# Where the modulation units and the first output-projection groups stand in two attention mixers

## The chip, the cores and the metric

One Trainium2 chip, one core. The kernel is a single launch; its time is device microseconds of that core, the median of three runs. TensorE (PE), ScalarE (ACT), VectorE (DVE), GpSimd (POOL) and the DMA queue of SyncE (SP) each take their instructions in program order and wait for each other on semaphores only. What is slow is therefore always one instruction at the head of an engine's queue, with everything behind it.

## The reference

The computation is three mixers in a row on 512 tokens of width 1024 (and, in the first two, 256 context tokens). Only the first two matter here:

```python
for i in range(2):                       # mixer A (i = 0), mixer B (i = 1)
    mod_x, mod_c = silu(c) @ w_mod[i] + b_mod[i], silu(c_ctx) @ w_mod[i] + b_mod[i]   # shift, scale, gate: 3 x 1024
    hx = rms_norm(x) * (1 + sc_x) + sh_x;  hc = rms_norm(ctx) * (1 + sc_c) + sh_c
    q, k, v, z = split(hx @ w_in)        # A: 16 query heads, 4 key heads, rope; B: 16 heads, window of the grid + bias
    o = softmax(q @ k.T * scale) @ v     # keys: tokens and context
    yx = (o * silu(z)) @ w_out
    x = x + g_x * yx                     # A also updates ctx, B does not
```

Then come a third mixer (recurrent heads and sparse attention) and a last norm, which the change leaves as they are.

## The kernel before

All weights go through one stream of units of 128 x 2048 numbers (1 MB each), in the order of `unit_order()`: unit n is loaded into buffer n % 2 of `W` when unit n - 2 has been used up. A projection in float32 is made of three fast matmuls: ACT rounds the weights to `WH`, POOL (or DVE) makes the rest `WL = W - WH` (`split`, four quarters a unit), and activations are kept as `HX`, `LX` (tokens) and `HC`, `LC` (context) in the same way. One slice `k` of a projection (`pj`) is WH*H, WH*L, WL*H. Modulation units (`mod_units`) are used as they are: `mod_mm` (16 matmuls from `W`), a copy of the sums by ACT (`mod_row`), `mod_tr` (4 small matmuls), one addition by DVE.

The order of the whole program is made by a planner in plain Python: `do(...)` appends an item, and every engine then walks the same list and issues its part of each item. In mixers A and B `attention()` interleaves two things. The steps are the attention itself: A has 48 steps, 8 pairs of heads by 6 tiles of 128 queries (tiles 0 to 3 have 768 keys, tiles 4 and 5 are context, with 256), B has 32, 8 pairs by 4 tiles with 512 keys. Step n issues the scores of n (PE), the softmax (DVE maximum, ACT exponential, DVE reciprocal, POOL scaling), the transposes of step n - 1 (`turn`) and the output of step n - 2 (`pv`). A generator, the fill, hands out projection work between these, at two places of each step: ahead of the second `turn` and ahead of the next step. A budget (`rate`, from `work` over the number of steps) says how much. `yield PAUSE`, or `yield -2`, ends the filling at this place, `until(...)` blocks it until a step has been planned.

```python
            def fill_in(n):
                debt[0] = min(debt[0], 60) + (rate * todo[n][2] if n < N else 0)
                while debt[0] > 0:
                    x = next(fill, None)
                    if x is None or x < 0:
                        break
                    debt[0] -= x
```

In A the fill is: for each pair the query projection (`gen_aq`, unit `aqz`, then the squares, sums and rope of the query), one modulation unit, the gate projection (`gen_az`); then three more modulation units and the activation parts of pairs 0 to 6. Parts (`parts`, by `parts_a`, `parts_b`) are what the output projection reads: ACT copies the gated attention output of pair k over slice k of HX and HC (possible only when the last gate projection has been read), and POOL (even k) or DVE (odd k) makes the low part. After the last step come the last gate, the parts of pair 7, two more modulation units, all splits of two weight units (`flush`), and then `out_proj`: the first two column blocks by both spans, four groups in four PSUM banks, first slices 0 to 5 of all, then 6 and 7 of each.

In B the fill is `gen_b(1)`, `gen_b(2)`, `gen_z(0)`, `gen_b(3)`, `gen_z(1..3)`, parts 0 to 5, where `gen_b(a)` projects queries, keys and values of the two pairs of group a and `gen_z(a)` their gates. `gen_b(a)` begins when group a - 2 is done with its buffers, `gen_z(a)` when group a is done. Its queries and keys have four buffers (`qB`, `kB`, by pair), its values two (`vB`, by group).

## Time and profile before

| what | value |
|---|---|
| runs | 1722.02 us median of 3 (1721.81 to 1722.54) |
| the profiled execution | 1719.79 us, of it 1718.1 us span |
| PE busy | 1584.9 us, 92% of the span |
| DVE, ACT, POOL busy | 729.3, 612.6, 643.1 us |
| mean granted TensorE clock | 0.954 |
| mixer A, first scores to last `pv` | 105.8 to 483.4 us |
| mixer B, first scores to last `pv` | 640.1 to 929.5 us |

The row of slices on the page gives each engine's busy share in tenths for 1/40 of the span (43 us); the row PEclk gives the granted TensorE clock. Where PE reads 9, the place is bound by TensorE; where it reads 5 to 8, TensorE waits for something, and a window of the trace tells for what.

### The profile page before, as it was taken

What the parts mean: (1) busy time and instruction counts of PE and PEld (TensorE: products, weight loads), DVE (VectorE), ACT (ScalarE), POOL (GpSimd) and SP (SyncE); (2) the same over time, 40 slices, a digit from 0 to 9 for tenths busy, and PEclk for the clock granted to TensorE, in tenths of its full rate; (3) what the DMA queues carried; (4) which work ended last, traced back from release to release, by engine and by line L of the source; (5) the groups of instructions that cost most, each with busy time, mean ns of one, the idle gap of its engine ahead of it and who ended that gap; (6) DMA issues with size and microseconds to landing.
All of it is one profiled execution on the core that took longest, in us unless ns stands there. A gap on an engine that the chain in (4) does not pass through costs nothing.

```text
span 1718.1 us, 25028 instructions
## 1 busy us (share of the span) xinstructions
PE 1584.9 (92%) x9858; PEld 1240.2 (72%) x9858; DVE 729.3 (42%) x1714; ACT 612.6 (36%) x1291; POOL 643.1 (37%) x640
## 2 busy tenths in 40 slices
PE   5899999999789799999997889999999898999997
PEld 3786677777568588788876668888887874555855
DVE  4344444444532624345355452524332374554033
ACT  4244444444522323333334342434332243333221
POOL 2433344342312434333343443435345242332352
PEclk8899999999979899999999889999998899999998
DMA  8111111111233222221221202122121221111221
GB/s 353 56 44 50 50 50 50 50 38 38 74 113 108 74 80 87 74 81 56 93 68 56 98 31 98 50 74 99 50 98 50 98 74 50 50 50 50 74 75 72
DMA packets 22148, 128.20 MB, mean 75 GB/s; under 512 B 2448, under 2 KB 2576, under 8 KB 8080
## 3 DMA queue, kind: packets, MB, share of 16 engines
q1 hardware_dynamic: 21888, 126.35, 20.6%
q8 instruction: 78, 1.28, 0.3%
q14 instruction: 38, 0.31, 0.1%
q10 hardware_dynamic: 144, 0.26, 0.1%
HBM read 124.50 MB, written 2.10 MB: 74 GB/s over the span
## 4 chain that ended last, share of the span: by engine, by line
PE 79%; DVE 9%; issue 4%; ACT 3%; POOL 3%; DMA 1%; DVEq 0%; POOLq 0%; SPq 0%; ACTq 0%
PE PS L1298 14%; PE PS L1300 14%; PE PS L1299 14%; PE PS L1379 6%; PE PS L1414 6%; PE PS L1389 5%; PE PS L1544 3%; PE PS L1293 3%; PE PS L1294 3%; PE PS L1295 3%; PE PS L1554 1%; DVE sm L1972 1%; POOL WL L2287 1%; ACT AR L1651 1%; DVE AR L2086 1%
## 5 line engine op out<-in xcount | busy, mean ns | idle before, releaser
L2287 POOL TENSOR_TENSOR WL<-W,WH 128x512 fp32r<-128x512 f32 x268 | 348.3, 1315 | 365.6 <-ACT WH L1574 365.3
L1298 PE MATMUL PS<-HX,WH 128*128 128x512 f32 x1008 | 414.7, 411 | 20.4 <-DVE LX L1895 16.9
L1300 PE MATMUL PS<-HX,WL 128*128 128x512 f32 x1008 | 398.1, 395 | 0.0
L1299 PE MATMUL PS<-LX,WH 128*128 128x512 f32 x1008 | 397.9, 395 | 0.0
L1298 PEld LDWEIGHTS PS<-HX,WH 128*128 128x128 f32 x1008 | 192.8, 191 | 68.9 <-issue 23.7
L1300 PEld LDWEIGHTS PS<-HX,WL 128*128 128x128 f32 x1008 | 192.0, 190 | 42.4
L1299 PEld LDWEIGHTS PS<-LX,WH 128*128 128x128 f32 x1008 | 192.8, 191 | 36.9 <-issue 1.9
L1574 ACT CAST WH<-W 128x512 fp32r<-128x512 f32 x296 | 171.0, 616 | 44.8 <-DMA W<-in_wu 37.4
L1651 ACT ACTIVATE AR<-PS,sm 128x768 f32<-128x768 f32 (+4 forms) x160 | 115.7, 723 | 177.8 <-DVE sm L1977 105.3
L1972 DVE TENSOR_REDUCE sm<-PS 128x1 f32<-128x512 f32 (+4 forms) x224 | 149.9, 669 | 42.5 <-PE PS L1379 38.1
L2343 POOL TENSOR_SCALAR AR<-AR,sm 128x768 f32<-128x768 f32 (+1 forms) x96 | 73.4, 764 | 220.8 <-DVE sm L1988 220.8
L1379 PE MATMUL PS<-AR 64*128 64x256 f32 (+3 forms) x704 | 126.9, 468 | 11.1 <-ACT XC L1651 5.2
L1414 PE MATMUL PS<-AR 128*64 128x128 f32 x1408 | 103.1, 295 | 21.9 <-DVE AR L1997 13.1
L1414 PEld LDWEIGHTS PS<-AR 128*64 128x64 f32 x1408 | 82.5, 146 | 49.8 <-issue 30.4
L1379 PEld LDWEIGHTS PS<-AR 64*128 64x128 f32 x704 | 61.0, 189 | 64.7 <-issue 41.5
L1389 PE MATMUL PS<-C,AR 128*128 128x128 f32 x608 | 101.8, 287 | 4.5 <-DVE AR L2008 4.1
L2343 POOL TENSOR_SCALAR XC<-XC,sm 128x512 f32<-128x512 f32 x64 | 44.8, 700 | 160.1 <-DVE sm L1988 160.1
L1661 ACT COPY AR<-PS 128x512 f32<-128x512 f32 (+1 forms) x112 | 62.1, 554 | 116.0 <-PE PS L1389 115.6
L1389 PEld LDWEIGHTS PS<-C,AR 128*128 128x128 f32 x608 | 70.1, 144 | 40.4 <-issue 25.1
L1293 PE MATMUL PS<-WH,HX 128*128 128x256 f32 x320 | 96.6, 302 | 2.6 <-POOL WL L2287 2.6
L1651 ACT ACTIVATE XC<-PS,sm 128x512 f32<-128x512 f32 x64 | 44.2, 690 | 149.1 <-DVE sm L1977 149.1
L1294 PE MATMUL PS<-WH,LX 128*128 128x256 f32 x320 | 93.2, 291 | 0.0
(268 smaller groups left out, 2488.4 us busy)
## 6 DMA issues: line engine op xcount, KB each, us to landing
W<-in_wu SPq DMA_DIRECT2D x98, 1024.0 KB, 4.8
AR<-in_wu SPq DMA_DIRECT2D x8, 1024.0 KB, 11.0
AR<-in_biasb SPq DMA_DIRECT2D x32, 256.0 KB, 2.7
XX<-in_xt SPq DMA_DIRECT2D x2, 1024.0 KB, 6.1
out<-XX SPq DMA_DIRECT2D x8, 256.0 KB, 2.2
XC<-in_xt SPq DMA_DIRECT2D x1, 1024.0 KB, 14.4
C<-in_cc SPq DMA_DIRECT2D x1, 770.5 KB, 8.6
CS<-in_cs SPq DMA_DIRECT2D x1, 512.0 KB, 9.9
```

Of the source, the lines that this page charges most:

```text
L1293: e.matmul(o, xh, wh, start=(k == 0), stop=False)
L1294: e.matmul(o, xl, wh, start=False, stop=False)
L1298: e.matmul(o, wh, xh, start=(k == 0), stop=False)
L1299: e.matmul(o, wh, xl, start=False, stop=False)
L1300: t = e.matmul(o, wl, xh, start=False, stop=(k == 7))
L1379: t = e.matmul(PS[:, s.score[h] + a:s.score[h] + b], l, r, start=True, stop=True)
L1389: t = e.transpose(o[:, j * 128:j * 128 + 128], s.pb[h][:, (q0 + j) * 128:(q0 + j) * 128 + 128], c("id"))
L1414: t = e.matmul(s.out[h], s.values[h][j], s.pt[h][:, j * 128:j * 128 + 128], start=(j == 0 and s.first), stop=(j == nv - 1 and s.final))
L1574: e.copy(WH[:, PART[n], a:z], W[:, n % 2, a:z]).then_inc(*s_wh.by(n, q))
L1651: e.activation(s.pb[h][:, 0:s.n], PS[:, s.score[h]:s.score[h] + s.n], ACT.Exp, bias=smn[:, i % 4:i % 4 + 1], scale=(1.0 if s.scale is None ...
L1972: e.tensor_reduce(mx, x, AX.X, ALU.max).then_inc(*s_max.by(name, n, h))
L2287: e.tensor_tensor(WL[:, d, a:z], W[:, n % 2, a:z], WH[:, d, a:z].bitcast(F32), ALU.subtract).then_inc(*s_wl_pool.by(n, q))
```

## The change

Mixer A: the modulation units are no longer fill of their own. `gen_aq` and `gen_az` take a second generator, `ride`, and step it once after each of their two spans: `mod_mm` and `mod_row` after the first, `mod_tr` after the second, so that a span's projection lies between the copy and the matmul that reads it. All twelve units of the fill ride in pairs 0 to 6 in this way (in `unit_order()` they stand between the `aqz` units accordingly); none is left behind the last step. In both mixers the output projection's first two column blocks of the token span begin within the fill (`begin_out`): after the parts of pairs 0, 1, 2 comes slice 0 of both, and so on to slice 6, each slice two behind the parts. After the last step follow the parts of pair 7, in A the two context groups (slices 0 to 6), then slice 7 of each. `flush()` ahead of the output projection is gone. Mixer B: queries and keys of pair m may be written when pair m - 4 is done, values of group a when pair 2a - 3 is done; the gates of group a come ahead of `gen_b(a + 2)` and no longer wait for the group's steps, as `b_gated` is issued when both the gate and the pair are there.

```diff
-    u = [("ak",), ("av",), ("aqz", 0)]
-    for i in range(7):
-        u += [("aqz", i + 1), m[i]]
-    u += m[7:12]
+    u = [("ak",), ("av",), ("aqz", 0), m[0]]
+    for i in range(1, 8):
+        u += [("aqz", i)] + m[2 * i - 1:2 * i + 1 if i < 6 else 12]
...
-        def gen_aq(pair, pr):
+        def gen_aq(pair, pr, ride=iter(())):
...
                 do("a_query_raw", pair, j)
+                next(ride, None)
                 yield PAUSE
...
+        def begin_out(name, phase, part, done, pr):
+
+
+            un = Unit(name, 0)
+            led = {(m, 0): bank(pr.take((name, m, 0), (s_res, (name, m, 0)))) for m in (0, 1)}
+            for k in range(9):
+                if k < 7:
+                    yield from until(lambda: k in done)
+                    part(k)
+                    yield 3
+                if k >= 2:
+                    for m in (0, 1):
+                        yield from pj((name, m, 0), un, 0, T, 128 * m, phase, led[m, 0], (k - 2,))
+            begun[name] = un, led
...
         def fill_a():
+            riding = iter(MA[:12])
...
             for pair in range(8):
                 if pair:
-                    yield from gen_aq(pair, FA)
-                    yield from mod_units(MA[pair - 1][0], (MA[pair - 1][1],), FA)
-                if pair < 7:
-                    yield from gen_az(pair, FA)
-            yield from gen_az(7, FA)
-            for l, u in MA[7:10]:
-                yield from mod_units(l, (u,), FA)
-            yield from parts_a(range(7))
+                    yield from gen_aq(pair, FA, ride())
+                yield from gen_az(pair, FA, ride())
+            yield from begin_out("aout", "o", parts_a, done_a, FA)
...
-        run(parts_a(range(7, 8)))
-        for l, u in MA[10:12]:
-            run(mod_units(l, (u,), FA))
-        flush()
+        LEAD = ring((2,), (3,))
+        parts_a(7)
...
         def gen_b(a, pr):
-            yield from until(lambda: a < 2 or a - 2 in done_b)
             for m in (2 * a, 2 * a + 1):
+                yield from until(lambda: m < 4 or m - 4 in pairs_b)
...
+            yield from until(lambda: a < 2 or 2 * a - 3 in pairs_b)
             un = Unit("bv", a)
...
-            yield from until(lambda: a == 3 or a in done_b)
+            yield from until(lambda: not a or 2 * a - 1 in gated_b)
...
-                  chain(gen_b(1, FB), gen_b(2, FB), gen_z(0, FB), gen_b(3, FB), gen_z(1, FB), gen_z(2, FB), gen_z(3, FB), parts_b(range(6))), 8 * (3 * (4 * T + 2 * LC + 6 * 256) + 8 * T) / 100 + 6 * 5,
+                  chain(gen_b(1, FB), gen_z(0, FB), gen_b(2, FB), gen_z(1, FB), gen_b(3, FB), gen_z(2, FB), gen_z(3, FB),
+                        begin_out("bout", "p", parts_b, gated_b, FB)), 8 * (3 * (4 * T + 2 * LC + 6 * 256) + 8 * T + 14 * T / 8) / 100 + 7 * 3,
                   posted_b, scored_b)
-        for m in (6, 7):
-            do("b_gated", m)
-        run(parts_b(range(6, 8)))
-        flush()
+        parts_b(7)
```

Where the instructions stand. TensorE in A, the end of step 43 and step 44 before: L1379 are scores (two spans, two heads), L1414 is `pv`, L1389 the transposes of one head, L1311 a `mod_mm`, L1320 its `mod_tr`.

```order
L1379 MATMUL PS<-AR 128x512 x2
L1379 MATMUL PS<-AR 128x256 x2
L1414 MATMUL PS<-AR 64x128 x12
L1389 MATMUL PS<-C,AR 128x128 x6
L1311 MATMUL PS<-W,sm 32x256 x8
L1389 MATMUL PS<-C,AR 128x128 x6
L1320 MATMUL PS<-C,AR 128x2 x2
```

TensorE in A with the change, step 42: L1398 are its scores, L1433 the `pv` of step 40, L1408 the transposes of step 41, and L1317 to L1319 slice 0 of the output projection for the first and the second column block.

```order
L1398 MATMUL PS<-AR 128x512 x2
L1398 MATMUL PS<-AR 128x256 x2
L1433 MATMUL PS<-AR 64x128 x4
L1408 MATMUL PS<-C,AR 128x128 x2
L1317 MATMUL PS<-HX,WH 128x512
L1318 MATMUL PS<-LX,WH 128x512
L1319 MATMUL PS<-HX,WL 128x512
L1317 MATMUL PS<-HX,WH 128x512
L1318 MATMUL PS<-LX,WH 128x512
L1319 MATMUL PS<-HX,WL 128x512
L1408 MATMUL PS<-C,AR 128x128 x2
```

So the modulation unit with its pair of matmuls has left this place, and the first output-projection slice now stands between the two transposes of a step, ahead of the second one.

ScalarE in A before, the end of the attention: L1615 are the copies of the parts (the last of the fourteen of pairs 0 to 6, then the two of pair 7), L1661 copies of transposes, L1651 exponentials, L1581 the modulation copies, L1574 the rounding of weights.

```order
L1615 CAST HC<-AR 128x256
L1661 COPY AR<-PS 128x512
L1651 ACTIVATE AR,sm<-PS,sm 128x256 x2
L1661 COPY AR<-PS 128x256 x2
L1615 CAST HX<-AR 128x512
L1615 CAST HC<-AR 128x256
L1581 COPY AR<-PS 128x256 x2
L1574 CAST WH<-W 128x512 x8
```

ScalarE in A with the change, step 42 and the beginning of step 43: the same copies of parts are L1634, the exponentials L1670, the copies of transposes L1680.

```order
L1670 ACTIVATE AR,sm<-PS,sm 128x768 x2
L1634 CAST HX<-AR 128x512
L1634 CAST HC<-AR 128x256
L1634 CAST HX<-AR 128x512
L1634 CAST HC<-AR 128x256
L1634 CAST HX<-AR 128x512
L1634 CAST HC<-AR 128x256
L1680 COPY AR<-PS 128x256
L1634 CAST HX<-AR 128x512
L1634 CAST HC<-AR 128x256
```

The fourteen copies stood in one block behind the exponentials of step 46 before; they now come in blocks of six, two, two, two and two, behind the exponentials of steps 42 to 44, and the eight roundings of weights and the modulation copies behind the last step are gone from there.

ScalarE in B with the change, steps 28 to 31: L1634 parts, L1670 exponentials (two heads), L1680 copies of transposes, L1593 the rounding of the next unit's weights.

```order
L1670 ACTIVATE XC,sm<-PS,sm 128x512 x2
L1634 CAST HX<-AR 128x512 x4
L1680 COPY AR<-PS 128x512
L1634 CAST HX<-AR 128x512
L1670 ACTIVATE XC,sm<-PS,sm 128x512 x2
L1634 CAST HX<-AR 128x512
L1593 CAST WH<-W 128x512 x2
L1634 CAST HX<-AR 128x512
L1680 COPY AR<-PS 128x512
L1670 ACTIVATE XC,sm<-PS,sm 128x512 x2
```

Before, the first six parts stood behind the exponentials of step 30 (two, a copy of a transpose, four); now the first five stand behind those of step 28.

## Rows read from the trace of the kernel before

**Rows 1.** The page: busy time of TensorE, its clock by slices, and one group.

```profile
PE 1584.9 (92%) x9858; PEld 1240.2 (72%) x9858; DVE 729.3 (42%) x1714; ACT 612.6 (36%) x1291; POOL 643.1 (37%) x640
PE   5899999999789799999997889999999898999997
PEclk8899999999979899999999889999998899999998
...
L2287 POOL TENSOR_TENSOR WL<-W,WH 128x512 fp32r<-128x512 f32 x268 | 348.3, 1315 | 365.6 <-ACT WH L1574 365.3
```

**Rows 2.** Windows: from:to length, busy of each engine, granted clock, DMA share, GB/s.

```profile
105.78:431.42 325.64, 306.23 (x2370) 234.61 (x2371) 150.57 (x417) 139.82 (x300) 124.05 (x126) 0.98 0.13 46
431.42:483.37 51.95, 36.75 (x314) 25.82 (x313) 27.54 (x65) 23.63 (x54) 18.70 (x20) 0.84 0.17 62
483.37:491.65 8.28, 5.77 (x42) 3.06 (x41) 3.46 (x9) 3.02 (x7) 0.00 (x0) 0.50 0.60 192
491.65:511.19 19.54, 19.54 (x96) 16.70 (x97) 6.00 (x10) 3.86 (x8) 0.00 (x0) 0.85 0.38 134
...
700.34:723.49 23.15, 19.77 (x113) 15.62 (x112) 8.84 (x26) 7.20 (x16) 7.85 (x8) 0.85 0.07 23
723.49:912.15 188.66, 188.66 (x1393) 157.47 (x1392) 91.99 (x240) 69.35 (x159) 72.00 (x75) 1.00 0.22 76
912.15:929.48 17.33, 8.23 (x74) 6.54 (x73) 9.02 (x20) 7.99 (x17) 8.51 (x8) 0.80 0.18 61
...
929.48:973.30 43.82, 43.81 (x194) 35.95 (x192) 18.30 (x27) 18.22 (x32) 16.48 (x13) 1.00 0.21 72
```

**Rows 3.** Waits of TensorE in 105.78:437.1: us in total, times, longest.

```profile
PE PS L1414 <- DVE AR L1997: 5.2, 6, 1.0
PE PS L1364 <- ACT AR L1633: 4.5, 3, 1.7
...
PE PS L1320 <- ACT AR L1581: 3.0, 2, 1.5
```

**Rows 4.** Timeline of TensorE in A, steps 43, 44: start, length, instruction [idle before].

```profile
437.12 1.56 PE L1379 MATMUL PS<-AR 64*128 64x512 f32 x8
...
447.98 1.07 PE L1311 MATMUL PS<-W,sm 128*32 128x256 f32 x16
448.98 0.87 PE L1389 MATMUL PS<-C,AR 128*128 128x128 f32 x6
451.15 0.58 PE L1320 MATMUL PS<-C,AR 128*128 128x2 f32 x4 [1.29 <-ACT AR L1581]
```

**Rows 5.** Timeline of TensorE in A, behind the scores of step 47.

```profile
474.15 2.83 PE L1414 MATMUL PS<-AR 128*64 128x128 f32 x24 [7.88 <-DVE AR L1997]
...
483.37 1.93 PE L1311 MATMUL PS<-W,sm 128*32 128x256 f32 x16
```

**Rows 6.** Timeline of ScalarE in A: the second exponential of step 42.

```profile
435.90 0.99 ACT L1651 ACTIVATE AR<-PS,sm 128x768 f32<-128x768 f32 x1 [0.56 <-DVE sm L1981]
```

**Rows 7.** Timeline of POOL and of DVE: low parts of activations.

```profile
466.01 1.26 POOL L2317 TENSOR_TENSOR LX<-AR,HX 128x512 fp32r<-128x512 f32 x1 [0.59 <-ACT HX L1615]
...
468.62 1.75 DVE L1902 TENSOR_TENSOR LX<-AR,HX 128x512 fp32r<-128x512 f32 x1
...
485.18 0.69 DVE L1902 TENSOR_TENSOR LX<-AR,HX 128x512 fp32r<-128x512 f32 x1 [0.35 <-ACT HX L1615]
```

**Rows 8.** Timelines in B: scores of steps 8, 29, 30, an exponential, `pv` of step 30.

```profile
706.90 2.08 PE L1379 MATMUL PS<-AR 64*128 64x256 f32 x8 [3.38 <-ACT XC L1651]
...
899.65 1.13 PE L1379 MATMUL PS<-AR 64*128 64x256 f32 x8
905.00 0.20 ACT L1651 ACTIVATION_READ_ACCUMULATOR XC<-PS,sm 128x1 f32 x1
908.27 1.13 PE L1379 MATMUL PS<-AR 64*128 64x256 f32 x8
...
923.96 1.97 PE L1414 MATMUL PS<-AR 128*64 128x128 f32 x16 [4.57 <-ACT AR L1661]
```

More of the change, by code:

```diff
@@ L58, in unit_order @@
     for a in range(4):
+        u += [("bz", a - 2)] if a >= 2 else []
         u += [("bqk", 2 * a), ("bqk", 2 * a + 1), ("bv", a)]
-        u += [("bz", a - 2)] if a >= 2 else []
     u += [("bz", 2), ("bz", 3)]
@@ L717, in gen_aq, with gen_az @@
             yield PAUSE
-        def gen_az(pair, pr):
+        def gen_az(pair, pr, ride=iter(())):
             un = aun[pair]
@@ L724, in gen_az @@
                 do("a_gate", pair, j)
+                next(ride, None)
                 yield PAUSE
@@ L786, in build @@
         unv.done(s_proj, "av", 5)
-        attention("a", [s for pair in range(8) for s in steps_a(pair)], SA, TA, PbA, PTbA, OA, fill_a(), 8 * 15 * (T + LC) / 100 + 14 * 5, posted_a)
+        attention("a", [s for pair in range(8) for s in steps_a(pair)], SA, TA, PbA, PTbA, OA, fill_a(), (8 * 15 * (T + LC) + 14 * T) / 100 + 7 * 3, posted_a)
         do("a_last_gate")
@@ L795, in out_proj @@
             for u in range(4):
[L796 to L797 removed]
                 if u == 0:
[L799 to L802 removed]
+                    un, led = begun[name] if name in begun else (Unit(name, 0), {})
+                    for j, (lo, hi) in enumerate(spans):
+                        for m in (0, 1):
+                            if (m, j) not in led:
+                                led[m, j] = bank(LEAD.take((name, m, j), (s_res, (name, m, j))))
+                                run(pj((name, m, j), un, lo, hi, 128 * m, phase, led[m, j], range(7)))
+                else:
+                    un = Unit(name, u)
                 for m in (2 * u, 2 * u + 1):
@@ L896, in gen_z, with gated, parts_b @@
                 do("b_gate", m)
-                if a < 3:
-                    do("b_gated", m)
+                gates_b.add(m)
+                gated(m)
                 yield 3
             un.done(s_proj, "bz", 2 * a + 1)
-        def parts_b(ks):
-            for k in ks:
-                parts("p", k, 0, zB[:, k, :], [(s_gated, ("b", k)), (s_proj, ("bz", 7))], "pool" if k % 2 == 0 else "dve")
-                yield 5
+        def gated(m):
+            if m in gates_b and m in pairs_b:
+                do("b_gated", m)
+                gated_b.add(m)
+        def parts_b(k):
+            parts("p", k, 0, zB[:, k, :], [(s_gated, ("b", k)), (s_proj, ("bz", 7))], "pool" if k % 2 == 0 else "dve")
         def load_bias(n):
```

42 lines of the change are left out of this document (19 added, 23 removed).

## The prediction

> **What bounds the kernel now.** I read the page first: TensorE is busy 92% of the span, and its row of slices reads 9 nearly everywhere but in a few dips, two of which lie where mixers A and B end, near 470 and 920 us; the clock row dips with it [rows 1]. So I asked for windows around these two ends, then for the waits and the timelines inside them.
>
> In A, from the first scores to those of step 42, TensorE is busy 306 of 326 us. Then it thins out: 36.8 of 52.0 us to the last `pv`, at a granted clock of 0.84, then 5.8 of 8.3 us in the last two modulation units at 0.50, then the first four output groups in 19.5 us at 0.85 [rows 2]. The end of these four groups, 511.19, is my mark of A. In B TensorE is full from 723 to 912 us. Ahead of that, the 23 us of steps 7 to 9 hold 3.4 us of idle at a clock of 0.85; behind it, 17.3 us hold 8.2 us of work. From 929.48 on it is full again [rows 2]: eight groups of eight slices in 43.8 us, 0.68 us a slice. My mark of B is the end of the first two output groups: sixteen slices, 940.4.
>
> So TensorE's own work sets the time nearly everywhere, and the change issues the same matmuls. All there is to win or lose is idle time and half-speed time: 19.4, 15.2, 2.5, 3.4 and 9.1 us of idle in these windows, 50 in all.
>
> **A, before step 42.** Five more modulation units now lie here (twelve for seven), and the second half of the last gate projection. A unit costs 1.0 us (`mod_mm`, to the transposes behind it) and 0.58 us (`mod_tr`) [rows 4], so 7.9 us; the projection's context span is 8 slices of half of 0.68, 2.7 us. Together +10.6. What goes: the waits for the modulation copy, 3.0 us, since a span's projection now lies ahead of `mod_tr`, and most of the 4.5 us that the query's sums wait for ACT, since in pairs 1 to 6 a `mod_tr` stands ahead of them; I take 3. The 5.2 us behind copies of transposes stay [rows 3]. A clock of 0.98 over 326 us is 6.5 us of full speed missing [rows 2], and it drops behind idle; I let 4 come back. What comes: the fill is less even. In the planner's new list the steps of tile 0 of pairs 3 to 6 get only 1.5, 0.8, 0.4 and 0 us of fill, at the prices above. Such a step needs 2.6 us of TensorE for itself (scores 1.5, context `pv` and transposes 1.1, estimated from a third of a full one), and step 42, the like of it, takes 5.7 us from 431.42 to 437.12 [rows 2, 4], with its fill. If 5.5 is the floor, 1.4 + 2.1 + 2.5 + 2.9 = 9 us are new idle. Against it, three steps that were thin, the ones behind the old modulation units, are full now; -3. Sum: 10.6 - 3 - 3 - 4 + 9 - 3 = +6.6. A second count, step by step (a step's work or its floor, plus the excess that its kind has in the trace), gives +4. I take +4, nearer to the count that uses more rows: the scores of step 42 at 435.5. The ends are 0 and +9.
>
> **A, from step 42 to the mark.** Before: 511.19 - 431.42 = 79.8 us. After:
> Step 42. The first slice waits for its part: the second exponential ends 5.5 us behind the scores' start (436.9) [rows 6], the copy takes 0.6, the low part by POOL 1.26 [rows 7]: 7.4 us, while TensorE is through with scores, `pv` and transposes after 2.4. A wait of 5.0 us. Then four slices, 2.7 us, and a transpose: 10.3. In B, 3.4 us of idle are followed by scores at half speed, 2.08 us for 1.13 [rows 8], so I add 1.5: 11.8.
> Step 43 holds three slices, and its chain sets it: 7. In step 44 the low parts of pair 5 on DVE stand ahead of its maximum, at 1.75 us for 512 columns with POOL at work, not 0.69 [rows 7]: 8. Step 45: 7. Step 46, short and without fill: 5.5. From the `pv` of step 45 to the end of the last one it took 9.2 us (474.15 to 483.37) at half speed [rows 5]; with the scores of step 47 ahead, 9.8. The 7.88 us that this `pv` waited behind fourteen copies of parts [rows 5] is gone. Sum 49.1.
> Then the context groups, 14 slices of 0.34, and slice 7 of all four: 6.8 us at full speed. The last gate and the parts of pair 7 lie beneath them, 3 us if they didn't. The old window from 491.65 lost 0.15 x 19.5 = 2.9 us to the clock [rows 2]; so does this: 9.7.
> 58.8 instead of 79.8: -21.0. With +4 ahead of it A gains 17.0.
>
> **B.** Steps 7 to 9: `bz` 0 waits for nothing now, and pair-wise buffers let the next projections follow. The 3.4 us of idle [rows 8] and the half speed, 0.15 x 23.15 = 3.5 us [rows 2], go: -6.9.
> The end: all gates are planned by step 27, not 30. So at the scores of step 28 the kernel has done what it had done at 912.15, less three attentions of 3.15 us (a step of 8.62 us, 899.65 to 908.27, less eight slices) [rows 8]: 902.7 on the old clock. From there to the mark took 37.7 us. After: step 28 waits for its first part as A does: exponentials end 5.55 us behind the scores (905.20) [rows 8], copy 0.6, POOL 1.3: 7.45, a wait of 4.8 us behind 2.6 us of work. Six slices and a transpose make 11.9, half speed 12.9. Step 29: slice 5 waits for part 5, 1.9 us, and slice 6 for part 6, whose low part stands on POOL behind two quarters of weights of 1.3 us [rows 1], 1.5 us: 11.2. Step 30: 5.5. Step 31: exponentials 5.5, then scaling, transposes, copy and `pv`, 3.3 as an estimate (rows 5 hold this piece twice in 9.2 us at half speed). Then nothing covers gate and part of pair 7, 2.3 us, where six slices a group did; two slices, 1.4. Sum 42.1, +4.4, though the 4.57 us behind the parts [rows 8] are gone. B gains 2.5.
>
> **Weights.** Without `flush` POOL spreads the next unit's splits, and the unit after is loaded some 10 us later against A's mark, and needed 12 us later still. I count 0; without that cover it is one load, under 5 us.
>
> **Sum.** -17.0 - 2.5 = -19.5. The profiled execution would go from 1719.8 to 1700.3, and the median, 2.2 us above it, from 1722.0 to 1702.5; I say 1703.
>
> **A rule against the change.** Low parts take 1.75 us on DVE beside POOL and 0.69 alone [rows 7]. My price for it is the 1 us more in step 44; paid in all five steps with parts, 42 to 44, 28 and 29, it is 5.
> The Trainium skill (SBUF — State Buffer, "Who interferes with whom") says that a DVE tensor_tensor with both inputs in SBUF contends with GpSimd's reads. By that rule, which the trace bears out, parts among the steps slow both engines that the softmax needs; it is part of rival 2.
>
> **The rivals.**
> 1. The ends close up further: the first slices wait 2 us instead of 5, and A's thin steps cost nothing. A 4 + 3 more, B 3 more: 1693. For it: TensorE's work alone would allow it. Against: both waits are read off a chain. 0.20.
> 2. The parts press on DVE and POOL: 5 us as above, and the clock is at half through both ends, 3 us more each: 1703 + 11 = 1714. For it: rows 7, and 0.50 in the old window from 483. 0.15.
> 3. Slower. TensorE stands in order: a slice that waits delays the transposes and scores behind it, these the next exponentials, and behind those stands the next part. If the other twelve parts wait too (three do in my sum), it decides from 19.5 / 12 = 1.6 us each; at 2.3 us it is 1703 + 28 = 1731. For it: parts are issued behind the exponentials of their step. Against: a slice stands two parts behind. 0.04.
> 4. The change doesn't do what it says: the waits only move into thin steps of A (+9 there, 13 less at its end), and B's end eats what step 8 gives: 1719 to 1723. 0.04.
> My forecast, 1697 to 1709: 0.57.
>
> **Range.** 1691 to 1714, with rival 1 and nearly all of rival 2. 0.2% (3.4 us) is about what a measurement can tell from no change. Faster 0.92, same 0.04, slower 0.04.
>
> **What would show it.** A: `mod_tr` without waits; scores of step 42 near 435; ahead of the first output slice a wait of 4 to 5 us for POOL's low part, and none near 7.9 us behind it; the mark near 494. B: no idle in steps 7 to 9 and a clock of 1.00 there; a wait of 4 to 5 us in step 28, two smaller ones in step 29, one of 2 us ahead of slice 7; the time between the marks 2 to 3 us shorter. It is wrong if A's thin steps lose more than 9 us, if the first waits drag the steps behind them, or if the clock stays at half through both ends, which the sum has at 1.5 and 2.9 us in A and 1 in B.
> The Trainium skill (TensorE: Matmul & The Clock Gate, "HAM oscillation — how this bites in real kernels") says that bursts with pauses between them bring the clock down again and again. The trace agrees behind the 3.4 us in B.

## The result: slower, where faster was predicted

The changed kernel takes 1755.69 us (median of 4 runs, 1747.64 to 1756.69) against 1721.91 us for the one before (1720.25 to 1722.54): a ratio of 1.0191, with a 95% interval of 1.0169 to 1.0212. Predicted were 1703 us, with a range of 1691 to 1714. The profiled execution took 1756.69 us, of it 1755.0 us span.

Its page, the rows that answer to [rows 1]: busy time, TensorE and its clock in 40 slices, the splits by POOL.

```profile
PE 1600.5 (91%) x9858; PEld 1250.6 (71%) x9858; DVE 718.1 (41%) x1702; ACT 612.4 (35%) x1291; POOL 658.7 (38%) x652
PE   5899987888979799999997978999999898999997
PEclk8899999899999899999998888999998899999998
L2306 POOL TENSOR_TENSOR WL<-W,WH 128x512 fp32r<-128x512 f32 x280 | 364.1, 1315 | 348.3 <-ACT WH L1593 348.3
```

The number of matmuls is the same, and TensorE is busy 16 us longer. The sixth to the tenth slice of TensorE, 220 to 440 us, were all 9 and now read 8, 7, 8, 8, 8: that is the body of A, not its end. The windows say how much. They answer to [rows 2]: A's first scores to those of step 42; on to the mark of A; B's first scores to those of step 28; on to the sums of the norm behind B's output projection (they stood at 975.61 before).

```profile
105.00:483.42 378.42, 335.23 (x2494) 254.25 (x2495) 152.02 (x423) 143.30 (x310) 128.24 (x129) 0.93 0.16 56
483.42:537.25 53.83, 44.16 (x325) 32.77 (x325) 27.55 (x70) 25.44 (x57) 22.45 (x24) 0.94 0.01 4
661.17:924.65 263.48, 263.48 (x1913) 221.02 (x1912) 119.51 (x326) 98.17 (x223) 103.82 (x108) 1.00 0.22 77
924.65:1011.84 87.19, 68.40 (x362) 53.63 (x361) 38.17 (x72) 32.03 (x63) 32.42 (x29) 0.86 0.16 53
```

| stretch | before | predicted change | after | measured change |
|---|---|---|---|---|
| A, scores of step 0 to step 42 | 325.6 | +4 | 378.4 | +52.8 |
| A, step 42 to its mark | 79.8 | -21.0 | 53.8 | -26.0 |
| B, scores of step 0 to step 28, same work before it | 269.4 | -6.9 | 263.5 | -5.9 |
| B, on to the norm's sums | 72.9 | +4.4 | 87.2 | +14.3 |

The third row of before is 902.7 less 633.3, the last 975.6 less 902.7, with the place 902.7 as the prediction worked it out (the work that the changed kernel has behind it at its step 28). The last column sums to 35.2; with 1.8 between the mark of A and B's first scores it is the 36.9 us of the span, but for a tenth. The prediction's +4.4 ended at its mark of B, 940.4; that stretch took 50.2 us in the change for 37.7, +12.5, and the rest of the +14.3 lies behind the mark. So two of four terms were right or better, one was 10 off, and one was off by 49.

What A's body waits for, TensorE in 105:483.4 (answers to [rows 3]); the waits of `mod_tr` for its copy are gone, as predicted. Transposes waited 3.8 us before, scores 2.4; the waits of projections (L1317) are new. The query's sums (L1383, 4.5 before) and `pv` (L1433, 5.2 before, 2.1 now) wait a little less.

```profile
PE PS L1408 <- DVE AR L2027: 11.4, 10, 3.1
PE PS L1317 <- POOL WL L2306: 8.2, 5, 1.8
PE PS L1398 <- ACT AR L1670: 8.1, 4, 2.2
PE PS L1317 <- DVE AR L1951: 4.5, 3, 2.2
PE PS L1317 <- DVE AR L1971: 4.2, 4, 1.6
PE PS L1383 <- DVE AR L1951: 3.9, 2, 2.1
```

In words: transposes (L1408) wait for the output's scaling on DVE; projections (L1317) for POOL's splits, and for DVE's copies of a query (L1951) and of a gate (L1971) out of the PSUM bank that they are to use; scores (L1398) for the exponential. Idle is 378.42 - 335.23 = 43.2 us for 19.4 before; and a clock of 0.93 over 378 us is about 26 us of full speed missing for 6.5. These two make some 43 of the 52.8; the added work of five units and half a projection was put at 10.6.

The largest single wait, 3.05 us, comes three times (steps 22, 28, 34). Here around step 28, the timeline of TensorE:

```profile
359.85 1.53 PE L1433 MATMUL PS<-AR 128*64 128x128 f32 x24
361.31 0.66 PE L1408 MATMUL PS<-C,AR 128*128 128x128 f32 x4
365.01 0.44 PE L1408 MATMUL PS<-C,AR 128*128 128x128 f32 x2 [3.05 <-DVE AR L2027]
```

DVE in the same time:

```profile
359.22 0.69 DVE L1962 TENSOR_TENSOR AR<-PS,CS 128x512 f32<-128x512 f32 x1
363.48 0.69 DVE L1965 TENSOR_TENSOR AR<-AR 128x512 f32<-128x512 f32 x1 [3.57 <-POOL AR L2355]
...
364.68 0.28 DVE L2027 SCALAR_TENSOR_TENSOR AR<-PS,AR 128x128 f32<-128x128 f32 x1
```

And POOL:

```profile
358.99 2.28 POOL L2350 TENSOR_TENSOR sm<-sm 128x12 f32<-128x12 f32 x1
361.25 0.90 POOL L2362 TENSOR_SCALAR AR<-AR,sm 128x768 f32<-128x768 f32 x1
362.12 1.26 POOL L2355 TENSOR_TENSOR AR<-AR,CS 128x512 f32<-128x512 f32 x1
```

Read it from the bottom. POOL takes the root of the query's sums (2.28), a scaling of the softmax (0.90), and then its part of the query's rotation (`a_query_rope`, 1.26). DVE stands 3.57 us for that part, inside its own part of the rotation. Behind the rotation in DVE's order are the maximum of the new scores and the scaling of the output of two steps ago (L2027), which empties bank 5; and the next transpose goes into bank 5. TensorE has 2.8 us of work, then nothing, and the seven slices that were to fill this step stand behind that transpose. The clock falls behind it: 0.75 over the 6.7 us from 365.01. Windows of the wait and of what follows:

```profile
361.90:365.01 3.11, 0.06 (x1) 0.00 (x0) 1.44 (x4) 0.80 (x2) 1.48 (x2) 1.00 0.00 0
365.01:371.72 6.71, 6.71 (x23) 5.35 (x24) 1.04 (x4) 1.60 (x5) 1.75 (x2) 0.75 0.00 0
```

### The profile page after: what moved, and what is told of

It is laid out like the page before. It is cut to its first block, busy times and chain, and to the rows that moved or that the text cites. A ratio compares the mean times of both kernels' runs of the same rounds, so it can differ in the third digit from the quotient of the medians.

```text
span 1755.0 us, 25015 instructions
## 1 busy us (share of the span) xinstructions
PE 1600.5 (91%) x9858; PEld 1250.6 (71%) x9858; DVE 718.1 (41%) x1702; ACT 612.4 (35%) x1291; POOL 658.7 (38%) x652
## 4 chain that ended last, share of the span: by engine, by line
PE 77%; DVE 10%; issue 4%; POOL 4%; ACT 3%; DMA 1%; DVEq 0%; POOLq 0%; SPq 0%; ACTq 0%
PE PS L1317 14%; PE PS L1318 13%; PE PS L1319 13%; PE PS L1398 6%; PE PS L1433 6%; PE PS L1408 6%; PE PS L1563 3%; PE PS L1312 3%; PE PS L1313 3%; PE PS L1314 3%; DVE sm L1991 2%; POOL WL L2306 2%; PE PS L1573 1%; DMA W<-in_wu 1%; PE PS L1330 1%
## 5 line engine op out<-in xcount | busy, mean ns | idle before, releaser
L2306 POOL TENSOR_TENSOR WL<-W,WH 128x512 fp32r<-128x512 f32 x280 | 364.1, 1315 | 348.3 <-ACT WH L1593 348.3
L1317 PE MATMUL PS<-HX,WH 128*128 128x512 f32 x1008 | 422.1, 419 | 44.1 <-DVE LX L1914 17.2
L1318 PE MATMUL PS<-LX,WH 128*128 128x512 f32 x1008 | 403.5, 400 | 0.0
L1319 PE MATMUL PS<-HX,WL 128*128 128x512 f32 x1008 | 403.0, 400 | 0.0
L1317 PEld LDWEIGHTS PS<-HX,WH 128*128 128x128 f32 x1008 | 196.5, 195 | 95.7 <-issue 35.0
L1319 PEld LDWEIGHTS PS<-HX,WL 128*128 128x128 f32 x1008 | 195.5, 194 | 43.5
L1593 ACT CAST WH<-W 128x512 fp32r<-128x512 f32 x296 | 171.5, 616 | 49.5 <-DMA W<-in_wu 42.1
L1670 ACT ACTIVATE AR<-PS,sm 128x768 f32<-128x768 f32 (+4 forms) x160 | 115.5, 722 | 192.6 <-DVE sm L1996 105.4
L1398 PE MATMUL PS<-AR 64*128 64x256 f32 (+3 forms) x704 | 127.6, 470 | 13.8 <-ACT AR L1670 11.2
L1680 ACT COPY AR<-PS 128x512 f32<-128x512 f32 (+1 forms) x112 | 62.1, 554 | 161.5 <-PE PS L1408 161.3
L1408 PE MATMUL PS<-C,AR 128*128 128x128 f32 x608 | 105.5, 294 | 13.2 <-DVE AR L2027 11.7
L1398 PEld LDWEIGHTS PS<-AR 64*128 64x128 f32 x704 | 61.4, 191 | 70.0 <-issue 41.7
L1408 PEld LDWEIGHTS PS<-C,AR 128*128 128x128 f32 x608 | 72.3, 148 | 49.4 <-issue 26.1
L1433 PE MATMUL PS<-AR 128*64 128x128 f32 x1408 | 99.5, 288 | 8.0 <-ACT AR L1680 7.9
L1433 PEld LDWEIGHTS PS<-AR 128*64 128x64 f32 x1408 | 79.2, 142 | 35.3 <-issue 31.6
L1670 ACT ACTIVATE XC<-PS,sm 128x512 f32<-128x512 f32 x64 | 44.1, 689 | 151.4 <-DVE sm L1996 151.4
## 6 DMA issues: line engine op xcount, KB each, us to landing
CS<-in_cs SPq DMA_DIRECT2D x1, 512.0 KB, 10.4
```

What stands on the lines that cost most here:

```text
L1317: e.matmul(o, wh, xh, start=(k == 0), stop=False)
L1318: e.matmul(o, wh, xl, start=False, stop=False)
L1319: t = e.matmul(o, wl, xh, start=False, stop=(k == 7))
L1398: t = e.matmul(PS[:, s.score[h] + a:s.score[h] + b], l, r, start=True, stop=True)
L1408: t = e.transpose(o[:, j * 128:j * 128 + 128], s.pb[h][:, (q0 + j) * 128:(q0 + j) * 128 + 128], c("id"))
L1433: t = e.matmul(s.out[h], s.values[h][j], s.pt[h][:, j * 128:j * 128 + 128], start=(j == 0 and s.first), stop=(j == nv - 1 and s.final))
```

## The experiments

For each run the table gives the stretches of its profiled execution, by the starts of scores and of the norm's sums: A0-42 and A0-24 from A's first scores to those of step 42 and 24; 42-B on to B's first scores; B0-28; 28-N on to the norm's sums; the rest. The ratios are to runs of the kernel before taken beside each run, whose medians lie between 1720.2 and 1722.5 us.

| run | A0-24 | A0-42 | 42-B | B0-28 | 28-N | rest | median us | ratio (95%) |
|---|---|---|---|---|---|---|---|---|
| before | 186.9 | 325.6 | 201.9 | 257.7 | 84.6 | 742.5 | | |
| the change | 219.5 | 378.4 | 177.8 | 263.5 | 87.2 | 743.1 | 1755.7 | 1.0191 (1.0169-1.0212) |
| 1 ride only | 184.7 | 335.5 | 185.5 | 258.2 | 84.7 | 740.1 | 1713.6 | 0.9950 (0.9932-0.9968) |
| 2 no ride | 194.9 | 346.6 | 191.3 | 263.5 | 88.0 | 741.5 | 1740.2 | 1.0123 (1.0085-1.0161) |
| 3 all of B | 186.7 | 326.8 | 201.7 | 263.5 | 88.1 | 740.4 | 1728.1 | 1.0029 (1.0015-1.0043) |
| 4 B's order | 186.7 | 326.7 | 201.7 | 262.9 | 86.2 | 741.1 | 1726.4 | 1.0027 (1.0014-1.0039) |
| 5 change, A's old number | 184.7 | 334.8 | 179.6 | 263.5 | 87.8 | 741.3 | 1715.5 | 0.9962 (0.9944-0.9979) |
| 6 before, A's new number | 194.9 | 349.6 | 201.6 | 257.8 | 84.6 | 742.5 | 1742.2 | 1.0113 (1.0088-1.0139) |
| 7 A only, old number | 184.7 | 336.7 | 179.3 | 258.2 | 84.8 | 740.9 | 1706.1 | 0.9914 (0.9894-0.9933) |
| 8 B spread | 186.8 | 325.5 | 201.9 | 258.4 | 81.7 | 738.3 | 1712.5 | 0.9947 (0.9929-0.9964) |
| 9 A old, B spread | 184.7 | 335.9 | 180.5 | 258.4 | 79.2 | 745.1 | 1702.6 | 0.9892 (0.9874-0.9911) |
| 10 change, A 1000 | 200.0 | 363.3 | 180.1 | 263.5 | 85.2 | 739.7 | 1739.4 | 1.0113 (1.0096-1.0130) |
| 11 A 960, B spread | 196.3 | 338.8 | 178.0 | 258.4 | 79.0 | 739.3 | 1700.7 | 0.9888 (0.9873-0.9902) |
| 12 A old, B 1200 | 184.7 | 334.2 | 180.6 | 261.0 | 85.9 | 740.2 | 1710.5 | 0.9943 (0.9929-0.9958) |
| 13 change, rotation later | 209.9 | 360.2 | 179.4 | 263.5 | 87.3 | 745.2 | 1743.5 | 1.0133 (1.0094-1.0172) |
| 14 no ride, rotation later | 186.8 | 322.8 | 191.5 | 263.5 | 87.8 | 740.7 | 1716.4 | 0.9970 (0.9955-0.9985) |
| 15 as 14, B spread | 189.7 | 325.8 | 191.2 | 258.4 | 80.1 | 741.0 | 1703.7 | 0.9892 (0.9875-0.9908) |

In the rows of before, 1, 6 and 7, B0-28 has 17 slices less in it than in the change, and 28-N that much more: for B compare the two together, 342.3 us before and 350.7 in the change. Where B is spread (8, 9, 11, 15) some slices are shifted in the same way, and where A's number differs the work done by step 24 or 42 differs a little: the change has 24 more small matmuls (eight context slices, some 3 us) behind it at step 42 than run 5.

**Runs 1 to 4: the parts alone.** My first theory was the one that the waits for PSUM banks suggest: that the riding units break the order of the two banks that A's projections take in turn, and lose its body by themselves. Run 1 is the kernel before with riding alone.

```diff
+                next(ride, None)      # in gen_aq and gen_az, behind each span
...
-                    yield from mod_units(MA[pair - 1][0], (MA[pair - 1][1],), FA)
```

> The kernel before with one part of the change: the modulation units ride on A's projections (with the order of the weight units that goes with it), no output slices in the fill, B as before. Theory 1, riding itself lengthens A's body (one PSUM bank is asked for again right behind each projection, weights of the next pair are split late, and the idle brings the clock down): scores of step 42 some 50 us later than before (near 484), TensorE's waits there 40 us and more, and since two modulation units behind the last step are gone, 30 to 45 us slower in all. Theory 2, the body is lengthened by something else of the change: step 42 within 10 us of 435, and the time within 10 us of before.

It is faster, 0.9950: the theory falls. Riding alone adds 9.9 us to A's body, about the 10.6 of the added work, and takes 16.4 off behind it. Run 2 is the change without riding (the old places of the units, all twelve in the fill).

> The change without riding: A's modulation units are fill of their own as before (all twelve ahead of the output slices), everything else of the change stays. Theory 1: scores of step 42 back at 431 (+-2), the time 25 to 50 us below the changed kernel. Theory 2: step 42 stays above 470. As the five late units take one step each, the output slices come only in step 47, so the end of A is worth less than in the change: its mark (end of the first four output groups) 505 to 515, as before.

It is slow, 1.0123, and has lost 21.0 us in A's body with no unit more there up to pair 7. Neither theory has it right: step 42 starts at 450.5, between the 431 of the one and the 470 of the other, and the time is 15 us below the change, not 25 to 50. So something else that the change brings slows A's body by itself. Run 3 has the A of before and all of B's part; run 4 of that only the pair-wise buffers and the earlier gates, with no output slice in the fill.

```diff
-chain(gen_b(1, FB), gen_b(2, FB), gen_z(0, FB), gen_b(3, FB), gen_z(1, FB), gen_z(2, FB), gen_z(3, FB), parts_b(range(6))) ...
+chain(gen_b(1, FB), gen_z(0, FB), gen_b(2, FB), gen_z(1, FB), gen_b(3, FB), gen_z(2, FB), gen_z(3, FB), parts_b(range(6))) ...
```

> A as before, B as in the change (buffers by pair, gates earlier, output slices in the fill). The two traces give B as 8 us longer (36.2 us late behind B against 27.9 ahead of it). If that is B's own doing: 1722 + 8 = 1730. If it came from what A left behind: 1716 to 1720.

> A as before; of the change in B only the buffers by pair and the earlier gates, the parts and the output projection behind the last step as before. My reading of the two traces: the idle and the half clock of steps 7 to 9 go and nothing is added, 6 to 7 us faster (1715). Rival: B's end becomes worse also without the output slices, since all fill is gone by step 28 and the last steps are bare: 1720 to 1724.

Both lose, 5 us by the ratios, run 4 against my own reading that it would gain 6 to 7; B takes 351.6 and 349.1 us for 342.3. The idle of steps 7 to 9 is gone in both, and both lose more than that at the end, run 4 with no output slice at all among the steps. TensorE there, in steps 29 to 31:

```profile
902.82 1.13 PE L1384 MATMUL PS<-AR 64*128 64x256 f32 x8 [1.81 <-ACT XC L1656]
905.85 1.98 PE L1419 MATMUL PS<-AR 128*64 128x128 f32 x16 [1.90 <-ACT AR L1666]
...
921.51 1.90 PE L1384 MATMUL PS<-AR 64*128 64x256 f32 x8 [2.50 <-ACT XC L1656]
...
929.30 1.98 PE L1419 MATMUL PS<-AR 128*64 128x128 f32 x16 [2.98 <-ACT AR L1666]
```

The `pv` take 1.98 us, where that of step 28 took 1.09. The gates that had covered these steps are done earlier, so the steps stand bare: the scores of steps 29, 30 and 31 each wait for an exponential (1.8, 3.4 and 2.5 us), and the granted clock is 0.84 over the 86.2 us, so that 27 us of them run at half clock. The 3.4 us of idle in step 8 had not been removed; they had been moved to the end, where they came back larger.

**Runs 5 and 6: one number.** In A the change also altered the last argument of `attention`, the work that the fill is said to hold: 1014.3 for 991.6, which gives each half step 11.74 units instead of 11.48. Run 5 is the whole change with the old number, run 6 the kernel before with the new one.

```diff
-        attention("a", ..., (8 * 15 * (T + LC) + 14 * T) / 100 + 7 * 3, posted_a)
+        attention("a", ..., 8 * 15 * (T + LC) / 100 + 14 * 5, posted_a)
```

> The change with one number put back: the work that attention A is told its fill holds, 991.6 as before instead of 1014.3. It sets how much fill each half step gets (11.48 and 11.74 units). The planner's lists say that with 1014.3 the fill of a pair runs out before the pair's last step is over: it meets its own gate (the query projection of pair p waits for pair p-2) in steps 18, 24, 30 and 36, and step 36 gets none; with 991.6 it never does. Theory R (the faster supply lost A's body): steps 0 to 42 take 335 to 340 us instead of 378, as in the kernel with riding alone (335.5), the waits of 3.05 us ahead of the transposes and of 2.2 us ahead of the scores go, and the clock is near 0.98; the end of A stays at 178 us to B's first scores, B stays at 351 us to the norm sums: 1712 to 1719 us. Theory S (riding together with the early output slices loses it, whatever the rate): 1745 to 1756.

> The kernel before with one number changed, A's fill told as 1014.3 instead of 991.6; nothing else. Theory R: the same gates are met in steps 18, 24, 30 and 36 as in the change; steps 0 to 42 take 342 to 350 us instead of 326 (the kernel without riding took 346.6), with three or four waits of 3 us ahead of the transposes and as many of 2.2 us ahead of scores; the end is at most 4 shorter: 1733 to 1745 us. Theory S (the rate is no cause): 1720 to 1724.

Both come out in the ranges of theory R, though its reason for them falls below: run 5 gets 40 us of the median back (43.6 in A's body of the profiled executions), and run 6 loses 20 to 24 with nothing else changed. TensorE's waits in the body of run 5, the largest of its kinds:

```profile
PE PS L1317 <- POOL WL L2306: 5.8, 5, 1.2
PE PS L1433 <- ACT AR L1680: 3.6, 1, 3.6
PE PS L1383 <- DVE AR L1951: 2.8, 2, 1.4
...
PE PS L1408 <- DVE AR L2027: 1.9, 6, 0.3
```

and its window:

```profile
106.70:441.50 334.80, 313.57 (x2470) 238.19 (x2471) 152.35 (x422) 141.34 (x308) 127.08 (x128) 0.98 0.17 61
```

The wait for the output's scaling (L1408) is 1.9 us for 11.4, idle is 21.2 for 43.2, and the clock is back at 0.98.

**Runs 7 and 8: the parts that pay.** Run 7 has A of the change with the old number, and B as before. Run 8 has A as before and all of B's part, with one number: B's fill is said to hold 1060 units, not 1403. The values of the next pairs are then pulled in where they are needed, and what is left lasts through step 31, with five to six slices a step.

```diff
-begin_out("bout", "p", parts_b, gated_b, FB)), 8 * (3 * (4 * T + 2 * LC + 6 * 256) + 8 * T + 14 * T / 8) / 100 + 7 * 3,
+begin_out("bout", "p", parts_b, gated_b, FB)), 1060,
```

> Mixer A as in the change (units ride, first output groups among the last steps) but with the old 991.6, mixer B as before. Theory R with theory E (A's end gives what was predicted, 178 us from step 42 to B's first scores for 186 with riding alone): B's first scores at 619 to 622, B 342.5 to the norm sums: 1703 to 1709 us, some 7 below the kernel with riding alone. If the early output slices cost on DVE and POOL what they save, it is 1711 to 1715, the same as riding alone.

> Mixer A as before, mixer B as in the change, with one number: the work that attention B is told its fill holds, 1060 instead of 1403. By the planner's list the fill, which ended in step 30 with one slice, lasts through step 31 with 5 to 6 slices a step, since the values of pairs 2, 4 and 6 are then pulled in at once where they are needed. Theory T (B's end is lost because steps 28 to 31 have too little work of TensorE in them, and the clock falls behind their waits): step 28 to the norm sums takes 75 to 79 us instead of 88, the time up to step 28 grows by at most 4 less what moved: together 340 to 345 us for 351.6, 1716 to 1722 us. Theory U (the waits for the first parts, and DVE and POOL busy with parts, lose it): 1725 to 1730, as with the number of the change.

Run 7 is as expected, 1706.1. Run 8, 1712.5, is faster than expected, though step 28 to the norm's sums takes 81.7 us, not 75 to 79; of the 14.5 us that its span is below that of run 3, 11.5 lie in B (340.1 for 351.6) and 2.1 in the rest, where the two programs are the same.

**Runs 9 to 12: together, and sizes between.** Run 9 puts both numbers into the change; 10 gives A 1000; 11 is run 9 with A at 960; 12 is run 9 with B at 1200.

> The change with both numbers: A's fill told as 991.6, B's as 1060. If the two losses are separate, it has the A of the run with A alone (1706 where before was 1722.5) and the B of the spread fill (10 below before): 1694 to 1700 us. If the two share something (the state of the clock, the weights that are loaded ahead), it is 1702 to 1710.

> The change with A's fill told as 1000, between 991.6 and 1014.3. By the planner's list the fill meets its gate in steps 30 and 36 alone. Theory R (what costs is the fill standing at its gate and the lumps behind it): up to the scores of step 24 A runs within 3 us of the kernel with 991.6, and loses 10 to 25 us from there to step 42: body 345 to 360, in all 1725 to 1740 us. Theory P (what costs is the rate itself, more fill in each half step): the loss grows evenly from step 0, 16 us in all, 7 to 9 of them before step 24.

> Both numbers again, but A's fill told as 960: the fill lags a half step behind that with 991.6 in most pairs, meets no gate, and lasts through step 47 with one slice left over. If only gates matter, A's body is 334 to 340 us as with 991.6, and the end gains what the steps 46 and 47 now cover, 1 to 3 us: 1692 to 1700. If a lagging fill brings waits of its own (the rope of a pair late for its first scores), 1703 to 1712.

> Both numbers, A 991.6, B's fill told as 1200: it ends with one slice in step 31, where 1060 holds 6 slices in step 31 and the number of the change ends in step 30. Theory T (what the last steps hold of TensorE's work decides): between the two, step 28 to the norm sums 83 to 87 us, and 3 to 8 us over the run with 1060. Theory U (waits for parts decide): as with the number of the change, 87 to 88.

Run 9 misses its 1694 to 1700 by 3: B's part gives 5.5 us over run 7 (337.5 for 343.0 in B), and the profiled execution loses 4 in the rest, where the code is that of run 7. Windows of run 9, its B and the piece of B from step 28:

```profile
622.50:960.00 337.50, 325.82 (x2273) 269.05 (x2273) 158.02 (x398) 129.19 (x286) 137.62 (x136) 0.99 0.22 74
880.80:960.00 79.20, 67.53 (x385) 52.87 (x385) 38.02 (x73) 33.46 (x66) 37.22 (x33) 0.98 0.17 58
```

TensorE's waits in the second:

```profile
PE PS L1317 <- POOL LX L2336: 6.9, 2, 4.8
PE PS L1317 <- DVE LX L1921: 1.7, 1, 1.7
PE PS L1433 <- ACT AR L1680: 0.8, 1, 0.8
```

The two waits for POOL's parts are the same 6.9 us as in the change; what went are most of the waits of the bare steps and of the half clock, 0.98 for 0.86. So theory T holds and U doesn't: the parts cost little beyond their waits. Run 12 lies between, as T has it.

Run 11, at 960, meets no gate either and has a body of 338.8 us; its 1700.7 us are the least of all runs, though run 9 can't be told from it by the intervals. But its first half shows that a lower number is not harmless: with less work done by step 24 it takes 196.3 us to get there, where 991.6 takes 184.7, and projections wait 9.4 us for the copy of a gate (L1971) out of their bank, for 1.0 in run 5. It gets most of this back behind step 24. So the time does not simply rise with the number; what counts is how the fill falls among the steps.

Run 10 is where theory R as I had put it fails. I had taken the loss for the fill standing at its own gate (`until`, the pair before last must be done). By the planner's list that happens in steps 18, 24, 30 and 36 with 1014.3, in 30 and 36 with 1000. But run 10 has lost 15 us by step 24. Nor does P hold, which wants an even loss of half that. Run 10 is within 0.2 us of run 5 at the scores of step 14; then a query's context slices come in two pieces, five in step 14 and three in 15, where run 5 has all eight in 15. TensorE of run 10 behind that:

```profile
232.32 1.99 PE L1383 MATMUL PS<-C,AR 128*128 128x2 f32 x12 [1.41 <-DVE AR L1951]
234.25 1.22 PE L1398 MATMUL PS<-AR 64*128 64x256 f32 x4
235.40 2.83 PE L1433 MATMUL PS<-AR 128*64 128x128 f32 x24
```

The query's sums wait for the copy of slices that ended just ahead of them, and the following scores and `pv` run at half clock (2.83 for 1.53). There the two lists differ in where the modulation unit and the first five context slices fall: a half step earlier in run 10.

**Runs 13 and 14: the rotation's place.** Both keep 1014.3 and all four stands at the gate. They add a pause that lets the query's rotation be planned in the first half of a step only.

```diff
...
             do("a_query_sums", pair)
             yield PAUSE
+            if pair and half[0]:      # half[0]: 1 in the second filling of a step
+                yield PAUSE
...
```

What the planner's list has for pair 4 (slices in the first and the second half of the step):

```
            the change               run 13                  run 5
step 21     sums   | rotation        sums     |              8        | sums
step 22     7      | 1               rotation | 8            rotation | 6
```

> The change with its 1014.3 and one more pause: the rotation of a pair's queries is planned in the first half of a step only. By the planner's list this moves those of pairs 4, 5 and 6 from the second half of steps 21, 27, 33 to the first half of steps 22, 28, 34, and the stands at the gate in steps 18, 24, 30 and 36 stay as they are. Theory Q (rotation ahead of the scores of a short step: its additions stand ahead of the output's scaling on DVE): the three waits of 3.05 us go and with them the half clock behind each, 5 to 6 us each: body 360 to 364 us instead of 378, 1737 to 1742 us. Theory G (the gate and the lumps behind it): 1750 to 1756.

> The same pause in the kernel without riding (1740 us, body 346.6, of which 21 are over the kernel before). Theory Q: its three waits of 3.05 us go, body 329 to 333, 1722 to 1727 us. Theory G: 1736 to 1741.

Theory Q holds in both. Run 13's body is 360.2 us, 18.2 less. The three waits of 3.05 us are gone. But not all of the 18.2 is the rotation: up to step 21 the change and run 13 issue the same instructions in the same order, and the change is 4.5 us behind there already (189.6 for 185.1), at a clock of 0.95 for 0.97: so much two executions can differ where nothing in them does. 13.7 us lie behind; steps 22, 28 and 34 alone give 10.4. The medians are 12.2 us apart, and their intervals just meet. Run 14 has 322.8, 24 less than run 2 (2.7 of it ahead of step 21) and less than the kernel before, with every stand at the gate still there: so without riding these stands cost nothing. The body of run 13:

```profile
106.00:466.20 360.20, 323.00 (x2495) 245.76 (x2496) 152.24 (x423) 143.01 (x310) 128.66 (x129) 0.97 0.17 59
```

and that of run 14:

```profile
103.80:426.60 322.80, 305.14 (x2394) 235.56 (x2394) 151.29 (x418) 140.37 (x300) 124.41 (x126) 0.99 0.14 47
```

Run 13 still has 25.4 us more than run 5. TensorE's waits in its body:

```profile
PE PS L1403 <- ACT AR L1675: 11.3, 8, 2.2
PE PS L1322 <- POOL WL L2311: 8.5, 5, 1.9
PE PS L1322 <- DVE AR L1956: 4.5, 3, 2.2
PE PS L1322 <- DVE AR L1976: 4.2, 4, 1.6
PE PS L1388 <- DVE AR L1956: 3.9, 2, 2.1
...
PE PS L1413 <- DVE AR L2032: 2.2, 7, 0.5
```

The wait behind the rotation (transposes, L1413) is 2.2 us for 11.4. The largest of the list, scores for exponentials, is 8.1 in the change; but it is not what sets run 13 apart from run 5, for these two differ by 25.2 us ahead of step 24 and by 0.2 behind it. Ahead of step 24 run 13 idles 20.8 us for 5.5, and of the 15.3 more, 13.0 are waits for splits (4.9 for 3.5), for banks (8.7 for 1.0) and of the query's sums for a copy (3.9 for none). The waits for splits and for banks, which run 14 doesn't have, have this reason: the riding unit takes the bank between a projection's two spans, so the second span finds its own bank not yet copied out when nothing else lies between.

**Run 15: the rest together.** The A of run 14 and the B of run 8.

> No riding, rotations in first halves, A's fill told as 1014.3, B's as 1060. If the two add up: the run without riding and with the later rotation was 4.6 below before, B's fill spread takes 337 to 340 us to the norm sums instead of 351: 11 to 14 less, so 1702 to 1706 beside a before of 1721. If B's part gives only the 4 us that it gave in the run with both old numbers: 1711 to 1714. The tail behind the norm sums 739 to 742 us as in nearly all runs, if the 745 of the run with both old numbers was that execution's own.

1703.7, with 741.0 in the rest. Runs 9, 11 and 15 are alike, 1.1% below the kernel before, with units that ride and without.

## Why the prediction was wrong, by its steps

**A, before step 42** ("I take +4") is the step that failed: +52.8. The runs take it apart, each piece one difference of the table:
- 9.2 us is riding and the added work, at the old number (run 5 less before). That was put at 10.6, and the waits of `mod_tr` did go. Of the 3 us taken off for the query's sums only 0.6 came: they waited 4.5 us before and 3.9 in the change.
- 18.2 us is the change less run 13. 13.7 of it lie behind the place where the two first differ and are the rotation, one half step too early in three pairs, give or take the 3 us or so by which executions differ; the other 4.5 lie ahead of it.
- 25.4 us comes with riding at the new number (run 13 less run 5, all of it ahead of step 24; seven context slices that run 5 does later, some 2.4 us, are in it); without riding, the same number and the same gates cost nothing (run 14 less before, -2.8). That the waits for splits and banks, and the clock behind them (0.98 for 1.00 up to step 24), make it up is read off the waits and not tried by itself.

I had the planner's list and counted in it only how much of TensorE's work each step holds, and took 9 us for the steps of tile 0 that get little. These, the stands at the gate, cost nothing by run 14, which has no riding; with riding they were not tried apart. What I didn't look at was in what order the query's copies, sums and rotation fall among the steps. Steps and fill share DVE's and POOL's queues, and there a rotation is a chain over POOL, 4.4 us from the root to the product in the rows above. [Rows 3] have such chains, 1 us each behind copies of DVE; I carried them over as they were. "I let 4 come back" of the clock has the wrong sign: 19 more went.

**A, from step 42 to the mark** was right in mechanism and small in size: 53.8 for 58.8. The first slice waited 5.01 us for POOL's part, where 5.0 was worked out,

```profile
490.95 0.77 PE L1317 MATMUL PS<-HX,WH 128*128 128x512 f32 x1 [5.01 <-POOL LX L2336]
```

and the 7.9 us behind the fourteen copies are gone. Steps 42 to 46 took 39.4 us where the sum has 39.3. The 5 us too many all lie behind the scores of step 47, where I had carried the half speed of before over: 7.1 us for 9.8 to the end of the last `pv`, and 7.3 for 9.7 in the groups behind it, at a clock of 0.94 from step 42 to the mark for 0.84, 0.50 and 0.85 before.

**B, steps 7 to 9:** -5.9 for -6.9, at a clock of 1.00 and without idle time. Right.

**B's end** was predicted at +4.4 to its mark and is +12.5 there, +14.3 to the norm's sums. The waits for parts came as worked out: 4.8 us in step 28, then 1.5 and 2.1 for 1.9 and 1.5, and 2.6 for 2.3 ahead of slice 7,

```profile
932.20 0.77 PE L1317 MATMUL PS<-HX,WH 128*128 128x512 f32 x1 [4.80 <-POOL LX L2336]
...
946.30 0.50 PE L1317 MATMUL PS<-HX,WH 128*128 128x512 f32 x1 [1.51 <-DVE LX L1921]
950.01 0.77 PE L1317 MATMUL PS<-HX,WH 128*128 128x512 f32 x1 [2.05 <-POOL LX L2336]
...
964.26 1.98 PE L1433 MATMUL PS<-AR 128*64 128x128 f32 x16 [2.98 <-ACT AR L1680]
973.44 0.80 PE L1317 MATMUL PS<-HX,WH 128*128 128x512 f32 x1 [2.56 <-DVE LX L1921]
```

By steps, 28 took 14.2 us for 12.9, 29 took 12.7 for 11.2, 30 took 6.6 for 5.5, and from the scores of step 31 to the mark it was 16.7 for 12.5. What I had at 1 us is the clock: 0.86 over 87.2 us is 12 us of full speed missing, and it is at its lowest, 0.52, in the last 12 us ahead of the mark. Spread over the steps (run 9), with the same two waits for POOL, less than 2 us of full speed are missing over 79.2 us.

The Trainium skill (TensorE: Matmul & The Clock Gate, "HAM oscillation — how this bites in real kernels") has a loop whose pauses bring the clock down each time anew, so that each costs more than its own length. The trace of the change agrees, 0.86 over this stretch; in the prediction I had cited the rule behind what would make the sum wrong, and had counted it with 1 us.

**The rivals.** None was this. Rival 4, that the waits move into thin steps, named the right place but priced it at 9. Rival 3, a chain of parts, didn't come. Of the later forecasts those for runs 2, 4 and 10 had no theory that fits. Those for runs 8, 9, 11, 13 and 14 were near but not inside: 1712.5 for at least 1716, 1702.6 for at most 1700, 1700.7 for at most 1700, 1743.5 for at most 1742, 1716.4 for at least 1722.

## What to carry to other kernels

A number that only paces a filler is part of the change, and it is the first thing to test alone: here 2.3% on it cost 40 us, more than the edit brought, and neither more nor less is safe (1014.3, 1000 and 960 each lost in A's first half, riding). When filler and steps share engines in program order, read where the filler's chains over several engines fall, not only how many matmuls each step holds; a chain whose end stands ahead of something that TensorE needs in the same step wants work behind it, or its place in the step pinned. And if work is drawn forward to fill a hole, look at the steps it came from: spread it by a lower pace rather than move it.

## What the runs showed of the hardware that was not expected

One wait of 3 to 5 us cost about 2 us of full speed behind it (0.75 over 6.7 us behind the 3.05 us above); where waits stand close together the clock fell again and more was lost. In the change the 4.80 us ahead of 932.20 lie at a granted clock of 0.71 and the 6.9 us behind them at 0.70; in run 9 a wait of 4.82 us at the same place lies at 1.00 and the 6.9 us behind it at 0.75. While TensorE works again that is 2.1 and 1.7 us of full speed missing, nearly the same. The difference comes later: from 904.40 on run 9 is at 1.00 to 960, while the change, whose next steps hold less work and more waits, falls again to 0.76 (950 to 957) and 0.52 (963 to 974.9). Windows of the wait and of what follows, in the change:

```profile
927.40:932.20 4.80, 0.00 (x1) 0.03 (x1) 2.95 (x7) 3.53 (x8) 2.11 (x3) 0.71 0.45 184
932.20:939.10 6.90, 6.90 (x24) 5.41 (x26) 2.16 (x3) 1.16 (x3) 3.53 (x3) 0.70 0.00 0
```

and in run 9:

```profile
892.68:897.50 4.82, 0.00 (x0) 0.03 (x1) 2.27 (x6) 4.00 (x9) 3.32 (x4) 1.00 0.12 14
897.50:904.40 6.90, 6.90 (x40) 4.95 (x41) 3.97 (x8) 1.12 (x3) 2.64 (x2) 0.75 0.35 142
```

Where the instructions are the same, stretches of different executions often repeat closely: steps 0 to 24 took 184.7 us in five runs with riding and the old number, 194.9 in both with the new number and no riding, and B's first 28 steps 263.5 in seven. But not always. Runs 14 and 15 issue the same instructions all through A, and its body took 322.8 and 325.8 us, at a clock of 0.99 and 0.98; runs 2 and 6, the same up to step 45, took 346.6 and 349.6; the change and run 13, the same up to step 21, took 189.6 and 185.1 us to there, at 0.95 and 0.97. The rest behind the norm's sums, the same work in all seventeen kernels, took 738 to 745 us. So a difference of 3 to 5 us between two profiled executions may be no more than that, and some kernels' own runs lie further apart (run 2, 1735.7 to 1749.5 us).
